# Joint attention layer of a two-block network in split fp32: values projected for all heads at once, scores of two heads issued in turn, stage borders overlapped

## What is computed

```python
x = x + y @ w_out_a                              # "w1": 2048 -> 1024
k, v = split(rms_norm(x, g_kv) @ w_kv, 2)        # "ak", "av": keys, values
q, z = split(rms_norm(x, g_b) @ w_qz, 2)         # "aq", "az": queries, gate
for c in range(8):                               # chunks of 64 queries
    s = q[c] @ k.T / 8 + bias                    # per head
    o[c] = softmax(where(valid, s, NEG)) @ v
x = x + (o * silu(z)) @ w_out_b                  # "w2": 1024 -> 1024
```

## Time and profile before

| | us |
|---|---|
| median of 3 runs | 1427.4 |
| the profiled execution | 1427.17 |
| its span, first to last instruction | 1425.4 |
| mean granted TensorE clock | 0.978 of full speed |

### The profile page before, as it was taken

How to read it: one execution, slowest core, us unless ns; L and a number is a source line. 1 busy time by engine, 2 the same in 40 slices (tenths; PEclk the granted TensorE clock), 3 DMA queues, 4 the chain that set the end, 5 groups by cost and what they waited for, 6 DMA issues and landing times.

```text
span 1425.4 us, 16281 instructions
## 1 busy us (share of the span) xinstructions
PE 1346.9 (94%) x6370; PEld 1108.4 (78%) x6370; DVE 716.8 (50%) x1280; ACT 647.9 (45%) x989; POOL 489.6 (34%) x206
## 2 busy tenths in 40 slices
PE   6999999999949999999899999999999999999985
PEld 5787888878837888888688778878887888878864
DVE  6455565542273444444346556777616456542225
ACT  4344444432235454455453656666545455552211
POOL 2454434334403323222142523333324232333430
PEclk9999999999979999999999999999999999999997
DMA  5632332343303222222133412222223232224321
GB/s 212 206 107 91 94 92 88 99 136 91 101 30 102 74 88 74 88 81 66 40 95 118 130 59 75 74 60 73 76 81 98 66 94 68 81 92 163 111 81 59
DMA packets 42157, 132.32 MB, mean 93 GB/s; under 512 B 6944, under 2 KB 9696, under 8 KB 41440
## 3 DMA queue, kind: packets, MB, share of 16 engines
q1 hardware_dynamic: 33120, 112.47, 25.1%
q10 hardware_dynamic: 8960, 18.81, 3.9%
HBM read 124.97 MB, written 10.49 MB: 95 GB/s over the span
## 4 chain that ended last, share of the span: by engine, by line
PE 85%; DVE 8%; ACT 4%; issue 2%; DMA 0%; POOL 0%; ACTq 0%; DVEq 0%; SPq 0%
PE banks L436 27%; PE banks L438 26%; PE banks L437 26%; PE banks L555 1%; DVE hd L1725 1%; DVE nfull L1375 1%; PE banks L830 1%; ACT L1180 1%; ACT L1179 1%; PE banks L797 1%; PE banks L676 1%; PE banks L527 0%; DVE hb L1722 0%; DVE nr L1367 0%; ACT hf L1182 0%
## 5 line engine op out<-in xcount | busy, mean ns | idle before, releaser
L426 POOL TENSOR_TENSOR wlo<-raw,whi 128x1024 fp32r<-128x1024 f32 (+2 forms) x202 | 489.4, 2425 | 900.3 <-ACT whi L915 900.3
L436 PE MATMUL banks<-hhi,whi 128*128 128x512 f32 x816 | 331.9, 407 | 18.4 <-DVE hlo L1379 15.9
L438 PE MATMUL banks<-hlo,whi 128*128 128x512 f32 x816 | 320.3, 393 | 0.0
L437 PE MATMUL banks<-hhi,wlo 128*128 128x512 f32 x816 | 320.0, 392 | 0.0
L915 ACT ACTIVATE whi<-raw 128x1024 fp32r<-128x1024 f32 (+2 forms) x202 | 210.0, 1042 | 224.1 <-PE banks L438 188.9
L436 PEld LDWEIGHTS banks<-hhi,whi 128*128 128x128 f32 x816 | 154.9, 190 | 52.0 <-DVE hlo L1379 16.7
L436 PE MATMUL banks<-yhi,whi 128*128 128x512 f32 x448 | 178.4, 398 | 6.9 <-DVE ylo L1506 3.5
L438 PEld LDWEIGHTS banks<-hlo,whi 128*128 128x128 f32 x816 | 154.4, 189 | 33.6
L437 PEld LDWEIGHTS banks<-hhi,wlo 128*128 128x128 f32 x816 | 154.9, 190 | 29.5 <-issue 1.9
L438 PE MATMUL banks<-ylo,whi 128*128 128x512 f32 x448 | 176.0, 393 | 0.0
L437 PE MATMUL banks<-yhi,wlo 128*128 128x512 f32 x448 | 175.6, 392 | 0.0
(11 more groups left out here) (345 smaller groups left out, 2124.4 us busy)
## 6 DMA issues: line engine op xcount, KB each, us to landing
raw<-w SPq DMA_DIRECT2D x194, 512.0 KB, 3.5
rel_tab<-relx ACTq DMA_DIRECT2D x1, 4096.0 KB, 19.0
tab<-rel_tab ACTq DMA_DIRECT2D x16, 224.0 KB, 3.3
x<-xt SPq DMA_DIRECT2D x4, 512.0 KB, 6.7
x<-xt ACTq DMA_DIRECT2D x1, 2048.0 KB, 8.3
x_kept<-x ACTq DMA_DIRECT2D x1, 2048.0 KB, 7.3
parts_kept<-mcg SPq DMA_DIRECT2D x8, 256.0 KB, 4.3
mgt<-parts_kept SPq DMA_DIRECT2D x8, 256.0 KB, 3.7
```

Source lines behind the costliest of these rows:

```text
L426: nc.gpsimd.tensor_tensor(wlo[:, n % 4, 0:width], raw[:, n % 2, 0:width], f32(whi[:, n % 4, 0:width]), ALU.subtract).then_inc(lo_done, 1)
L436: nc.tensor.matmul(dst, a[0], b[0], start=first, stop=False)
L437: nc.tensor.matmul(dst, a[1], b[0], start=False, stop=False)
L438: return nc.tensor.matmul(dst, a[0], b[1], start=False, stop=last)
```

## The change

- **Values.** The eight slabs "av" are now cut by tokens: `at_values(half)` projects the values of four pairs (512 columns) for all four groups of 128 tokens at once, into banks 4 to 7, with the tokens' tiles as the stationary operand. They come out with tokens on the partitions, as the attended outputs need them, so `avf` and its transposes go. The first half works on x·gain without the token factor (cut into `hhi`, `hlo` during "w1"), and the eviction multiplies by the factor; the second half works on the normalized tiles.
- **Norm.** The token factor is computed on a 128x4 column form, spread with a diagonal and one matmul with ones into bank 3; the 16 normalized tiles are written to `yhi`, `ylo` while TensorE does the first half of the values.
- **Scores.** Both heads' twelve matmuls are issued in turn (head 0, head 1, head 0, ...), always into different banks. Both heads' transposes then follow the next pair's keys; the cuts of a head's transposes are one instruction of 1280 columns instead of three.
- **Borders.** "w1" starts without the last tiles of "uz" and waits for each tile as it needs it. Of "w2", seven eighths of the first three slabs are done between the last pair's transposes and outputs.
- **Tables** are loaded on SP's queue, ahead of a later weight slab.

The reference's result and the number of slabs stay. The core of the diff (semaphore lists, buffer declarations and ScalarE's order of cuts are shortened):

```diff
+W2B = (0, 1, 3, 2)
-    order += [(name, h) for h in range(PAIRS) for name in ("ak", "aq", "av", "az")]
+    order += [("av", n) for n in range(TT)] + [("ak", 0), ("aq", 0)] + [("av", TT + n) for n in range(TT)] + [("az", 0)]
+    order += [(name, h) for h in range(1, PAIRS) for name in ("ak", "aq", "az")]
...
+AB = (2 * S, 5 * S + 2 * P)
+AK = ((0, S, 2 * S, S + KW[1]), (2 * P + S, 2 * P, 0, 2 * P + KW[1]))
+AQ = [[AK[q][TT - 1 - t] for t in range(TT)] for q in range(2)]
...
 SP, before the load of slab n
+                    if n == AT["av", 2]:
+                        sp.wait_ge(st_rel, 16)
+                        sp.wait_ge(atM.sem, atM.all())
+                        table(q, q)
+                    for i in range(PAIRS - 1):
+                        if n == AT["az", i] + 7:
+                            sp.wait_ge(asV.sem, asV.at(f"max{q}", i))
+                            table(q, 2 * i + 2 + q)
...
 TensorE
-            pe.wait_ge(uzV.sem, uzV.all())
-            pe.wait_ge(uzA.sem, uzA.all())
+            pe.wait_ge(uzA.sem, uzA.at("u0", 7))
+            for m in range(KT):
+                if m == 0:
+                    pe.wait_ge(uzV.sem, uzV.at("ylo1", 3))
+                if m == 1:
+                    pe.wait_ge(uzA.sem, uzA.all())
+                if m >= 2:
+                    pe.wait_ge(w1V.sem, w1V.at("x", m - 2))
+                slab("w1", 2 * m, bank[2 * (m % 2)], y_lower, last=False)
+                for k in range(KT):
+                    if m == 0:
+                        pe.wait_ge(uzV.sem, uzV.at(f"ylo{k % 2}", 4 + k // 2))
+                    slab("w1", 2 * m + 1, bank[2 * (m % 2)], y_upper, first=False, ks=[k])
+            def at_values(half):
+                for j in range(4):
+                    n = AT["av", 4 * half + j]
+                    pe.wait_ge(lo_done, n + 1)
+                    for k in (2 * j, 2 * j + 1):
+                        if half == 0:
+                            pe.wait_ge(w1V.sem, w1V.at("lo", k))
+                        else:
+                            pe.wait_ge(nbV.sem, nbV.at(f"lo{k}"))
+                        for t in range(TT):
+                            if half == 1 and k == 0:
+                                pe.wait_ge(avV.sem, avV.at(f"lo{t}", 0))
+                            a = [u[:, k, t * P:(t + 1) * P] for u in (h, y_lower)[half]]
+                            b = [u[:, n % 4, (k % 2) * S:(k % 2 + 1) * S] for u in (whi, wlo)]
+                            done = mm3(bank[4 + t], a, b, k == 0, k == KT - 1)
...
+                        if half == 0 and k == 0:
+                            pe.wait_ge(w1V.sem, w1V.at("acc", KT - 1))
+                            for t in range(TT):
+                                tok = nc.tensor.matmul(bank[1][:, t:t + 1], nacc[:, t * P:(t + 1) * P], ones[:, 0:1],
+                                                       start=True, stop=True)
+                        if half == 0 and k == 1:
+                            pe.wait_ge(nbV.sem, nbV.at("diag"))
+                            nc.tensor.matmul(bank[3], ones, adiag, start=True, stop=True).then_inc(nbP.did("wide"), 1)
+            def at_scores(i):
+                pe.wait_ge(akV.sem, akV.at("qlo", i))
+                if i >= 1:
+                    pe.wait_ge(auV.sem, auV.at("plo1", i - 1))
+                for t in (1, 2, 0, 3):
+                    if t == 3 and i >= 1:
+                        pe.wait_ge(auV.sem, auV.at("y0", i - 1))
+                    for a, b, first, last in ((qhi, khi, True, False), (qlo, khi, False, False), (qhi, klo, False, True)):
+                        for q in range(2):
+                            rows, c = slice(BD * q, BD * (q + 1)), AB[q] + AQ[q][t]
+                            done = nc.tensor.matmul(banks[:, c:c + QW[t]], a[rows, t * P:(t + 1) * P], b[rows, 0:QW[t]],
+                                                    start=first, stop=last)
...
+            at_values(0)
+            for i in range(PAIRS):
+                slab("ak", i, bank[0], y_lower, tiles=nbV if i == 0 else None)
+                if i >= 1:
+                    at_turned(i - 1)
+                    pe.wait_ge(asA.sem, asA.at("z", i - 1))
+                slab("aq", i, bank[1], y_upper, tiles=nbV if i == 0 else None, offset=KT)
+                if i == 0:
+                    at_values(1)
+                    pe.wait_ge(avV.sem, avV.at(f"lo{TT - 1}", 1))
+                else:
+                    at_attended(i - 1)
+                at_scores(i)
+                slab("az", i, bank[1], y_upper)
+            done_keys, last_key = range(KT - 1), [KT - 1]
+            pe.wait_ge(auV.sem, auV.at("ylo", PAIRS - 2))
+            slab("w2", 0, bank[0], h, ks=done_keys)
+            at_turned(PAIRS - 1)
+            pe.wait_ge(asA.sem, asA.at("z", PAIRS - 1))
+            slab("w2", 1, bank[1], h, ks=done_keys)
+            at_attended(PAIRS - 1)
+            slab("w2", 2, bank[3], h, ks=done_keys)
             pe.wait_ge(auV.sem, auV.all())
+            for m in range(3):
+                slab("w2", m, bank[W2B[m]], h, ks=last_key)
+            slab("w2", 3, bank[W2B[3]], h)
...
 ScalarE, in "w1": after each square
+                nc.scalar.activation(hhi[:, m, :], x[:, m, :], ACT.Copy, scale=col("kv_g", m)).then_inc(w1A.did("hi"), 1)
 ScalarE, the norm: 16 copies, with cut() at k = 0, 4, 8, 11 and at_values(0), the evictions of the values, at k = 12
 ScalarE, a round: cut, keys, both phi copies, cut, queries, cut, exponentials of both heads, silu
 VectorE, a round: keys, both plo, queries, outputs of the pair before, then
+            def probabilities(i):
+                dve.wait_ge(asP.sem, asP.at("s1", i))
+                for q in range(2):
...
+                for q in range(2):
+                    dve.wait_ge(asA.sem, asA.at(f"exp{q}", i))
...
```

More of the change, by code:

```diff
@@ L311, in build @@
                     + [name for k in range(1, KT) for name in (f"full{k}", f"lo{k - 1}")] + [f"lo{KT - 1}"]))
-        nb = norm_steps("nb", 2 * KT, True)
+        nbP = steps("nb_pe", ["tok", "wide"])
+        nbA = steps("nb_act", ["root"] + numbered("hi", 2 * KT))
+        nbV = steps("nb_dve", ["mean", "inv", "diag", "full0"]
+                    + [name for k in range(1, 2 * KT) for name in (f"full{k}", f"lo{k - 1}")] + [f"lo{2 * KT - 1}"])
         n2P = steps("n2_pe", ["tok", "wide"])
@@ L608, in values @@
+            slab("w2", 3, bank[W2B[3]], h)
+            for m in range(4, KT):
+                pe.wait_ge(w2V.sem, w2V.at(f"x{m - 4}"))
+                slab("w2", m, bank[W2B[m % 4]], h)
             def values(half):
@@ new lines, in _ @@
+            act.wait_ge(nbV.sem, nbV.at("inv"))
+            nc.scalar.activation(rt1[:, 2, :], rt1[:, 1, :], ACT.Sqrt).then_inc(nbA.did("root"), 1)
+            cut()
+            for k in range(2 * KT):
+                if k in (0, 4, 8, 11):
+                    cut()
+                if k == 12:
+                    at_values(0)
+                act.wait_ge(nbV.sem, nbV.at(f"full{k}"))
+                to = yhi[:, k, :]
+                nc.scalar.activation(to, nfull[:, k % 3, :], ACT.Copy).then_inc(nbA.did(f"hi{k}"), 1)
@@ L1094, in _ @@
+            keys(0)
+            cut()
+            queries(0)
+            for _ in range(4):
+                cut()
+            at_values(1)
+            cut()
+            weights_of(0)
+            for i in range(1, PAIRS):
+                cut()
+                keys(i)
+                turned(i - 1)
+                cut()
+                queries(i)
+                cut()
+                weights_of(i)
+            turned(PAIRS - 1)
             for m in range(KT):
@@ L1348, in _, with squares, sq @@
             act.wait_ge(mgV.sem, mgV.all())
+            def squares(a, v):
+                for m in range(KT):
+                    cut()
+                    if m:
+                        sq(a, v, m - 1)
+                sq(a, v, KT - 1)
+            def sq(a, v, m):
+                act.wait_ge(v.sem, v.at(f"x{m}"))
+                if m >= 2:
+                    act.wait_ge(v.sem, v.at(f"acc{m - 2}"))
+                nc.scalar.activation(nsq[:, m % 2, :], x[:, m, :], ACT.Square).then_inc(a.did(f"sq{m}"), 1)
             squares(w3A, w3V)
@@ L1597, in _ @@
[L1597 to L1609 removed]
+            dve.wait_ge(ld_x1, 16)
@@ L1611, in _ @@
+            at_values(0)
+            keys(0)
+            queries(0)
+            at_values(1)
+            probabilities(0)
+            for i in range(1, PAIRS):
+                keys(i)
+                turned(i - 1)
+                queries(i)
+                dve.wait_ge(asA.sem, asA.at("z", i - 1))
+                outputs(i - 1)
+                probabilities(i)
+            turned(PAIRS - 1)
+            dve.wait_ge(asA.sem, asA.at("z", PAIRS - 1))
+            outputs(PAIRS - 1)
             V.tensor_tensor(g12[:, :], vec[:, VEC["fin1"]:VEC["fin1"] + KT], vec[:, VEC["n2_g"]:VEC["n2_g"] + KT],
```

414 lines of the change are left out of this document (176 added, 238 removed).

## The result

| | before | after |
|---|---|---|
| median, us | 1428.0 (4 runs) | 1377.97 (4 runs, 1375.53 to 1383.16) |
| the profiled execution, us | 1427.17 | 1376.47 |
| its span, us | 1425.4 | 1374.7 |
| mean granted TensorE clock | 0.978 | 0.989 |

The ratio is 0.9657, 95% interval 0.9633 to 0.9681: faster by 50 us. The forecast was 1373.5 with a range of 1366 to 1387. That it came so near is partly luck: two errors of opposite sign stand in it. The scores gained 4.7 us more than forecast, and a stage that the change does not touch gave 9.8 us back.

The account below looks back on a forecast made before the run. TensorE, busy 94% of the span, was taken as the bound. Terms 5.0 + 26.0 + 9.4 + 4.4 - 3.1 + 12.0 = 53.7 us off 1427.2 gave 1373.5 us, range 1366 to 1387.

Parts of the forecast that it names:

- Start of "w1": Border before "w1": 3.48 us of TensorE idle and 1.5 of slow clock go, gain 5.0 us.
- The norm: Around the norm, TensorE's idle times, wide ones-matmul and slow clock go, covered by unnormalized values: gain 26.0 us.
- The cover of the last query tiles: In the norm, last normalized tile ready near 33 us, last query tile wanted at 33.8; margin one to three microseconds.
- Values by tokens: Eight slabs and transpose groups, 48.0 us, give way to 192 matmuls, 43.6 us: gain 4.4 us.
- Additions: One wide matmul, four narrow ones and a 1.41 us wait before the first scores: minus 3.1, bounds 2.5 to 6.
- Steady round: Attention rounds in the new order: three new waits are covered and priced at nothing; rounds of 25.2 us.
- the three new waits: Transposes wait for both softmaxes, outputs for both cuts, last score quarter for head 0's gated output; all priced at nothing.
- Scores in turn: Both heads' alternated score matmuls take 2.7 us per round instead of 4.2: gain 1.5 per round, 12.0 us.
- a pair that runs together but loads one after the other: Score pairs: two weight loads at 0.107 us each make a pair cost at least 0.214 us.
- full overlap: Rival on the scores: pairs cost as one, loads included, gain 16.8 instead of 12.0, 1368.7 us; chance 0.22.
- The end: Around the last outputs, idle 4.03 + 1.98 and slow clock go, covered by pieces of "w2": gain 9.4 us.
- a short wait: Rival: each round waits at transposes, outputs, last score quarter or late weights, 9.8 us in all, 1383.3 us; chance 0.13.

Follow-up runs that it names:

- blocks of three: Changed kernel with scores issued as three matmuls of head 0, three of head 1, and so on: 1375.93 us, ratio 0.9640 to the kernel before.
- GpSimd's work cut short: Changed kernel with GpSimd making the low part of only 128 of 1024 columns for seven weight slabs, work left out: 1368.36 us, ratio 0.9593.
- head by head: Changed kernel with all twelve score matmuls of head 0 issued before all twelve of head 1: 1389.76 us, ratio 0.9744.
- blocks of six: Changed kernel with scores issued as six matmuls of head 0, six of head 1, twice: 1384.81 us in one run.

## Why the prediction was nearly right, point by point

- *Start of "w1"*, 5.0: measured 5.4 (3.7 from the last transposes to "w1", 1.7 within it), and 4.9 when undone alone. Right.
- *The norm*, 26.0: right. From 394.00 to 452.11 TensorE has one idle time, the forecast 1.41. The cover of the last query tiles, called the thinnest, held.
- *Values by tokens*, 4.4: right. The slabs and transposes that went had the same rows as forecast, and what the 192 new matmuls need over 0.227 each is counted in the next line.
- *Additions*, -3.1: 1.8 in the first half (0.82 for the narrow matmuls, 0.46 for the wide one, the rest in longer distances behind both), 1.41 for the wait, and 0.4 of slower spacing between, 3.6.
- *Steady round*, nothing for the three new waits: right, no idle time in any of them. The round is 24.68 and not 25.2 for the scores alone.
- *Scores in turn*, 12.0: mis-sized. 4.21 less 2.12 per round is 16.7. The step that failed is "a pair that runs together but loads one after the other": the loads run in pairs, 0.11 us apart and not 0.21. The spacing of 0.107 was that of loads into the same rows, and I carried it over to different rows. The rival "full overlap", and with it the rule of the Trainium skill, "TensorE: Matmul & The Clock Gate", Part 3, had this right. The same part says that matmuls start strictly in program order; here the runs in blocks of three and six differ, and the measurement decides.
- *The end*, 9.4: right at its place. The old stretch from the transposes to the end of "w2", with the ten transposes that moved there added, was 58.1 + 1.1 us, and the new one 632.55 to 682.17, 49.6: 9.6. Its later part failed. I priced VectorE's bookkeeping of three slabs that finish together only through the fourth slab's weights ("at worst 1 us is lost"), and took 0.7 to 0.9 us for each step as if GpSimd were not there. The additions beside it took up to 2.88, and the stage behind gave 9.8 back; with GpSimd's work cut short 9.6 came back. Of the rivals none named this: a short wait was looked for inside the rounds.
- The sum: 5.4 + 26.0 + 9.6 + 4.4 - 3.6 + 16.7 - 9.8 = 48.7, against 50.7 measured between the profiled executions. Of the 2 us between them 0.4 stand before the last transposes of "uz", 1.1 between there and the second block, and 0.5 in the second block; none is assigned.

## What to carry to other kernels

When a change makes one engine finish several pieces at once, follow the pieces to the engines that book them, one stage beyond the edit, and ask whether those engines share something with a third. Steps of VectorE with two SBUF tiles beside a busy GpSimd can cost four times their row, and many such steps in a row can hold GpSimd up for longer still; one operand in a free PSUM bank avoids it. Before a difference of a few microseconds is put down to an edit, look whether such a collision, far from the edit, fell the other way. Two products of 64 rows are worth issuing near each other, on different halves and banks.

## What the runs showed of the hardware that was not expected

- Twelve pairs of 64-row matmuls, loads included, took 2.12 us, and twelve single ones 2.11, with 128 to 512 columns.
- A matmul on the other half of the rows started before three older ones (head by head, in blocks of six), and blocks of three ran as full pairs, 2.13 us.
- VectorE's additions of two SBUF tiles took up to 2.88 us instead of 0.68 beside a GpSimd subtraction, and 0.68 when one operand was in PSUM. A GpSimd subtraction took 6.63 us instead of 2.40 beside nine such steps in a row.
- TensorE's clock was at 0.50 of full in the 6.55 us that followed 5.68 us of standing still.
